# Cross attention's keys and values computed inside the third layer's mixer, with scores in five banks and keys feature-major

## The chip, the core and the metric

The kernel runs on one core of a Trainium2 chip. The metric is the device time of one launch in microseconds (us), the median of several runs. A core has five engines that run side by side, each through its own list of instructions in order, and that wait for one another by semaphores: TensorE (PE, matmul; PEld is its weight load), VectorE (DVE), ScalarE (ACT), GpSimd (POOL) and SyncE (SP, which here only issues the loads of weights). Matmul results land in PSUM, eight banks of 512 fp32 columns on 128 partitions; everything else lies in SBUF.

## What is computed

Three layers of a decoder over 512 tokens of width 1024, in fp32. The first two (A and B) are not touched by the change. The third, C, is the `second_block` of the reference:

```python
h = rms_norm_2(x, g_mix)
u, q, k, v, gate_logits = split(h @ w_in)
y_pool = causal_multiscale_pool(u, w_pool, pool_scale)
q, k = apply_rope(q), apply_rope(k)              # 4 heads x 2 halves of 64
o = diff_attention(q, k, v, lam)                 # softmax(half 0) - lam * softmax(half 1)
o = rms_norm_2(o, g_subln) * (1.0 - lam_init)
mixed = concatenate([y_pool, o]) * sigmoid(gate_logits)
x = x + mixed @ w_out
hc = rms_norm_2(x, g_cross)
mem_n = rms_norm_2(mem, g_mem)                   # 256 tokens of a memory
k, v = split(mem_n @ w_ckv)                      # 4 heads of 256
x = x + (softmax((hc @ w_cq) @ k.T) @ v) @ w_co
x = x + square(relu(rms_norm_2(x, g_mlp) @ w_up)) @ w_down
```

`mem_n @ w_ckv` needs nothing of x: its operands are inputs of the launch.

## The kernel before

All matrices of weights are cut into units of 1024 x 256 (1 MB), numbered in the order of `PHASES` (line 50). SP loads unit after unit into two buffers STG0 and STG1; ACT writes the high part of the unit (`split_hi`, WH) and DVE the rest (`split_lo`, WL), also into two buffers each. A product is three matmuls: high x high, low x high and high x low (`product`, line 472 is the matmul helper). A unit of a projection has 48 matmuls of 128x512. Semaphore `lo` says that a unit is split, `tile` that PE has finished a tile, `emptied_dve` or `emptied_act` that the tile's bank has been read. Unit u+2 can't be split until PE is through with unit u, and its load waits for the `lo` of unit u.

Layer C runs through the units C.u, C.qk, C.v, C.gate (in the projections DVE turns queries and keys by the rope), then the mixer (`layer_c_mixer`, no weights), then C.out, C.mem, C.cq, the cross attention, C.co and the MLP.

The mixer goes head by head, four heads h, with this chain for each:

- PE `scores(h, c)`: scores of half c, four query blocks of 128 (widths 128 to 512, 1280 columns), contraction over 64 rows. Half 0 lies in banks 0 to 2, half 1 in banks 3 to 5 (`1536 * c + DF_OFF[b]`). Of head 0 the two halves alternate, of the others all of half 0 comes first. The scores of half c of head h+1 wait until ACT has taken the exponentials of half c of head h.
- DVE `top(h, c)`: adds the causal mask, takes the row maxima, scales them (tile DMX).
- ACT exponentials (tile Y), with the row sums into DST.
- DVE difference: four scalar_tensor_tensor over Y.
- PE `turn(h, r)`: ten 128x128 transposes (line 1070) in three pieces r into bank 7; ACT copies each piece to UT; PE `apply(h, r)` multiplies by the values into bank 6.
- ACT copies the head to QC and its square to SQ.

Around it, four pooled groups (`UT,PAR` matmuls into banks 6 and 7, DVE scales them into GC_) fill the start; at the end 16 small matmuls sum the squares, and `head_factors` spreads the factors inside C.out's first unit, whose second half waits for the heads' operands.

C.mem has 8 units of 48 matmuls of 128x256: the memory's token tiles (MH2, ML2) are the stationary operand and the weights move, so the results are token-major. Units 0 to 3 are keys: ACT copies them to Y scaled by the tokens' factors, PE transposes them (line 1237) and ACT copies the transposes to CK. Units 4 to 7 are values, scaled by ACT into CV. The operand MH2, ML2 and the squares are made by ACT, DVE and POOL beside C.out, the operand of C.cq beside C.mem.

Of the kernel before, what the change touches and what calls it, by code (L numbers as in the profile page):

```python
# [26 lines left out]
F32R = mybir.dt.float32r  # L27
# [4 lines left out]
P = 128  # L32
# [20 lines left out]
    ("C.u", 2, "dve"), ("C.qk", 4, "dve"), ("C.v", 2, "dve"), ("C.gate", 4, "dve"), ("C.out", 4, "dve"),  # L53
    ("C.mem", 8, "act"), ("C.cq", 4, "dve"), ("C.co", 4, "dve"), ("C.mlp", 32, "dve"),
# [5 lines left out]
UNITS = len(KIND)  # L60

# [3 lines left out]
SPLITS = ["mem", "A.in", "A.mix", "A.mlp", "B.in", "B.mix", "B.mlp", "C.in", "C.mix", "mem2", "C.cross", "C.att", "C.mlp"]  # L65
# [41 lines left out]
rope_mm rope_sin rows_hi rows_in rows_tr rq rs rsc rv sb_a sb_az sb_cap sb_e sb_l sb_m sb_o sb_rc sb_sp sb_half sb_t sb_u sb_z  # L107
# [5 lines left out]
def program(nc, ws, xt_in, memt_in, memt2_in, par_in, con_in, rope_in, rcnt_in, out):  # L113
    ctx = ExitStack()
    with ctx:
# [40 lines left out]
        MX2 = KVM  # L156
        PS = ctx.enter_context(nc.psum_tensor("PS", [P, 8, 512], F32))
# [49 lines left out]
        with ExitStack() as sc:  # L207
            QC = sb("QC", [P, 4, S], scope=sc)
            KC = sb("KC", [P, 4, S], scope=sc)
            VC = sb("VC", [P, 4, NB, P], scope=sc)  # L210
            UT = sb("UT", [P, 4, 16 + S], scope=sc)
            GC_ = sb("GC_", [P, KD, S], scope=sc)
            COSIN = sb("COSIN", [P, 2, S], scope=sc)
            LAM = sb("LAM", [P, 8], scope=sc)
            PA = sb("PA", [P, 2, 16 + S], scope=sc)
            DST = sb("DST", [P, 5, 4 * NB], scope=sc)
            DMX = sb("DMX", [P, 2, 2, NB], scope=sc)
        with ExitStack() as sc:
            CQ0 = sb("CQ0", [P, 4, S], scope=sc)
            MH2 = sb("MH2", [P, KD, MEM], F32R, scope=sc)  # L220
            ML2 = sb("ML2", [P, KD, MEM], F32R, scope=sc)
        with ExitStack() as sc:
            CQ = sb("CQ", [P, KD, S], scope=sc)
            CQ_END = sb("CQ_END", [P, 4, S], scope=sc)
            CK = sb("CK", [P, KD, MEM], scope=sc)
            CV = sb("CV", [P, MB, D], scope=sc)
# [100 lines left out]
        NORMS = [n for n in SUMS if not n.startswith("mem")]  # L327
# [140 lines left out]
        def _(pe):  # L468
# [23 lines left out]
            def spread_tokens(name):  # L492

                pe.wait_ge(sems["rsc"], sums_done(name))
                for b in range(NB):
# [557 lines left out]
            def layer_c_mixer():  # L1053
                def scores(h, c):
                    pe.wait_ge(sems["df_exp"], 8 * (h - 1) + 4 * c + 4)
                    for b in (3, 2, 0, 1):
                        o = 1536 * c + DF_OFF[b]
                        last = mm(PSF[:, o:o + DF_WID[b]], QC[64 * c:64 * c + 64, h, b * P:(b + 1) * P],
                                  KC[64 * c:64 * c + 64, h, 0:DF_WID[b]], True, True)
                    last.then_inc(sems["df_s"], 1)  # L1060
# [25 lines left out]
                for b in (3, 2, 0, 1):  # L1086
                    for c in range(2):
                        o = 1536 * c + DF_OFF[b]
                        last = mm(PSF[:, o:o + DF_WID[b]], QC[64 * c:64 * c + 64, 0, b * P:(b + 1) * P],
                                  KC[64 * c:64 * c + 64, 0, 0:DF_WID[b]], True, True)  # L1090
                        if b == 1:
                            last.then_inc(sems["df_s"], 1)
                for g in range(4):
                    pe.wait_ge(sems["pool_z"], g + 1)
                    if g >= 2:
                        pe.wait_ge(sems["mixed"], g - 1)
                    elif g == 1:
                        pe.wait_ge(sems["rope_sin"], 8)
                    mm(PS[:, 6 + g % 2, :], par("w_pool", g * P, P), UT[:, g, 16:16 + S], True, True).then_inc(sems["pool_mm"], 1)
                for h in range(4):  # L1100
                    if h < 3:
                        scores(h + 1, 0)
                        scores(h + 1, 1)
# [8 lines left out]
                    apply(h, 2)  # L1112

                pe.wait_ge(sems["df_sq"], 4)
# [105 lines left out]
            rope_projection("C.gate", [[2, 3], [4, 5], [6, 7], []])  # L1220
# [3 lines left out]
            for r in range(4):  # L1224
                memory_rows(U0["C.mem"] + 2 * r, MH2, ML2, "mem2" if r == 0 else None)
                if r == 0:
                    sum_tokens("mem2", MB)
                memory_rows(U0["C.mem"] + 2 * r + 1, MH2, ML2)
                if r in (1, 2):

                    pr = r - 1
                    pe.wait_ge(sems["emptied_act"], emptied("act", U0["C.mem"] + 2 * pr + 1, 1))
                    if pr:
                        pe.wait_ge(sems["kv_t"], 4)
                    for f in range(4):
                        for t in range(MB):
# [1435 lines left out]
```

## Time and profile before

| | us |
|---|---|
| median of 3 runs | 2255.85 |
| range of the runs | 2253.93 to 2257.2 |
| the profiled execution | 2253.49 |
| its span in the trace | 2251.7 |
| PE busy, share of the span | 95% |
| DVE, ACT, POOL busy | 49%, 33%, 7% |

A stage's length is read from where PE's instructions begin and end. Start and length of each instruction are in microseconds from the span's start. Matmuls overlap, so the distance from start to start counts, not the length of one.

### The profile page before, as it was taken

How to read it: one execution, taken by the hardware profiler on the slowest of the kernel's cores; microseconds unless marked ns; L12 is line 12 of the kernel's file. 1: busy time of each engine (PE TensorE's matmuls, PEld its weight loads, DVE VectorE, ACT ScalarE, POOL GpSimd, SP SyncE). 2: the span in 40 equal slices, each digit the busy share in tenths (PEclk: the TensorE clock that was granted, in tenths of full speed). 3: DMA queues.
4: the chain of work that ended last, by engine and by line, in shares of the span. 5: the costliest groups of instructions: out<-in, count | busy, mean ns of one | idle time of the engine just before them, and what ended most of it. 6: DMA issues, size and time to landing. Idle time of an engine off the chain costs nothing.

```text
span 2251.7 us, 28790 instructions
## 1 busy us (share of the span) xinstructions
PE 2146.6 (95%) x11831; PEld 1757.9 (78%) x11831; DVE 1097.8 (49%) x1381; ACT 752.4 (33%) x1038; POOL 155.3 (7%) x137
## 2 busy tenths in 40 slices
PE   7999999899999999999999999899789999999998
PEld 6877888788888778767788888687469868888886
DVE  4664654454354353452744435555745334454453
ACT  5443432422122232673312213312435243222222
POOL 2000220200000210001100000300001001000001
PEclk9999999999999999999999999999889999999999
DMA  6231000122222222102222222322104302222221
GB/s 233 75 115 45 22 11 15 70 100 98 93 93 93 94 75 75 38 1 75 75 94 105 99 94 93 122 94 75 38 20 143 119 20 94 94 94 99 106 93 56
DMA packets 27025, 182.81 MB, mean 81 GB/s; under 512 B 2992, under 2 KB 3120, under 8 KB 5424
## 3 DMA queue, kind: packets, MB, share of 16 engines
q1 hardware_dynamic: 25200, 174.07, 21.8%
q10 hardware_dynamic: 1296, 4.71, 0.5%
q0 software_dynamic: 432, 2.62, 0.3%
q8 instruction: 74, 1.21, 0.2%
q14 instruction: 23, 0.19, 0.0%
HBM read 179.30 MB, written 2.10 MB: 81 GB/s over the span
## 4 chain that ended last, share of the span: by engine, by line
PE 86%; DVE 8%; ACT 3%; DMA 1%; issue 1%; POOL 0%; ACTq 0%; DVEq 0%; POOLq 0%; SPq 0%
PE PS L472 85%; ACT Y L1254 2%; DVE HL L1888 2%; DVE Y L1888 1%; DVE PS L1888 1%; DVE XT L1891 1%; DVE WL L1891 1%; ACT WH L1254 1%; DVE Y L1891 1%; DMA MX<-mem_t 0%; DVE SQ L1891 0%; PE PS L1070 0%; DMA STG<-weights 0%; PE PS L641 0%; POOL SQA L412 0%
## 5 line engine op out<-in xcount | busy, mean ns | idle before, releaser
L472 PE MATMUL PS<-HH,WH 128*128 128x512 f32 x1608 | 643.0, 400 | 32.4 <-DVE HL L1888 26.0
L472 PE MATMUL PS<-HL,WH 128*128 128x512 f32 x1608 | 632.1, 393 | 0.0
L472 PE MATMUL PS<-HH,WL 128*128 128x512 f32 x1608 | 631.6, 393 | 0.0
L1891 DVE TENSOR_TENSOR WL<-STG,WH 128x2048 fp32r<-128x2048 f32 (+1 forms) x167 | 376.3, 2253 | 286.5 <-ACT WH L1254 286.5
L1254 ACT ACTIVATE WH<-STG 128x2048 fp32r<-128x2048 f32 (+1 forms) x167 | 313.9, 1880 | 529.3 <-PE PS L472 527.8
L472 PEld LDWEIGHTS PS<-HH,WH 128*128 128x128 f32 x1608 | 305.4, 190 | 112.5 <-issue 28.7
L472 PEld LDWEIGHTS PS<-HH,WL 128*128 128x128 f32 x1608 | 305.4, 190 | 65.2
L472 PEld LDWEIGHTS PS<-HL,WH 128*128 128x128 f32 x1608 | 305.8, 190 | 62.7 <-issue 1.7
L472 PE MATMUL PS<-UPH,WH 128*128 128x512 f32 x768 | 299.1, 389 | 1.4 <-DVE UPL L1888 1.4
L472 PE MATMUL PS<-UPL,WH 128*128 128x512 f32 x768 | 298.8, 389 | 0.0
L472 PE MATMUL PS<-UPH,WL 128*128 128x512 f32 x768 | 298.8, 389 | 0.0
L472 PEld LDWEIGHTS PS<-UPH,WH 128*128 128x128 f32 x768 | 144.2, 188 | 31.6 <-DVE UPL L1888 1.8
L472 PEld LDWEIGHTS PS<-UPL,WH 128*128 128x128 f32 x768 | 144.2, 188 | 29.9
L472 PEld LDWEIGHTS PS<-UPH,WL 128*128 128x128 f32 x768 | 144.2, 188 | 29.9
L408 POOL TENSOR_TENSOR SQA<-SQ 128x512 f32<-128x512 f32 (+1 forms) x14 | 23.9, 1707 | 1695.6 <-ACT SQ L1254 1695.6
L1888 DVE SCALAR_TENSOR_TENSOR RR<-PS,RS 128x512 f32<-128x512 f32 x96 | 66.3, 691 | 152.6 <-PE PS L472 144.4
L1891 DVE TENSOR_TENSOR Y<-Y,PS 128x512 f32<-128x512 f32 x64 | 43.9, 687 | 180.2 <-PE PS L472 180.2
L1254 ACT ACTIVATE UPH<-RR 128x512 fp32r<-128x512 f32 x64 | 40.5, 632 | 233.5 <-DVE RR L1888 233.5
L1891 DVE TENSOR_TENSOR XT<-XT,PS 128x512 f32<-128x512 f32 x80 | 54.4, 682 | 125.9 <-PE PS L472 125.9
L412 POOL TENSOR_TENSOR SQA<-SQA,SQ 128x512 f32<-128x512 f32 (+1 forms) x70 | 94.8, 1354 | 134.9 <-ACT SQ L1254 131.0
L1254 ACT ACTIVATE Y<-PS 128x512 f32<-128x512 f32 (+5 forms) x96 | 61.6, 646 | 85.1 <-PE PS L472 70.3
L472 PE MATMUL PS<-WH,MH 128*128 128x256 f32 x192 | 56.3, 293 | 12.6 <-DVE ML L1888 9.2
(291 smaller groups left out, 2127.2 us busy)
## 6 DMA issues: line engine op xcount, KB each, us to landing
STG<-weights SPq DMA_DIRECT2D x163, 1024.0 KB, 4.8
XT<-x_t ACTq DMA_DIRECT2D x2, 1024.0 KB, 12.4
out_t<-Y SPq DMA_DIRECT2D x8, 256.0 KB, 2.0
STG<-weights SPq DMA_DIRECT2D x4, 256.0 KB, 5.7
MX<-mem_t ACTq DMA_DIRECT2D x4, 256.0 KB, 8.3
CON<-consts ACTq DMA_DIRECT2D x1, 1024.0 KB, 17.2
Y<-recip_counts POOLq DMA_DIRECT2D x1, 1024.0 KB, 5.1
KVM<-mem_t POOLq DMA_DIRECT2D x1, 1024.0 KB, 7.2
```

Of the source, the lines that this page charges most:

```text
L408: pool.tensor_tensor(SQA[:, 0:n], SQ[:, base % 4, 0:n], SQ[:, (base + 1) % 4, 0:n], ALU.add).then_inc(sems["sqa"], 1)
L412: pool.tensor_tensor(SQA[:, 0:n], SQA[:, 0:n], SQ[:, (base + k) % 4, 0:n], ALU.add).then_inc(sems["sqa"], 1)
L472: return pe.matmul(o, l, r, start=start, stop=stop, **kw)
L1254: return act.activation(o, i, f, **kw)
L1888: return dve.scalar_tensor_tensor(out=o, in0=a, scalar=s_, in1=b, op0=op0, op1=op1)
L1891: return dve.tensor_tensor(o, a, b, op)
```

## The change

Units are numbered so that C.mem comes before C.out. Each of its 16 half units (`memory_part(r, t)`, 24 matmuls of 128x256) stands in PE's list between steps of the mixer and writes its half of bank 5: both parts of unit 0 between the pooled groups, the first part of unit 1 ahead of head 1's scores and the second after `turn(0, 0)`; from head 1 on one part of unit 2h+1 after `turn(h, 0)` and the other after `apply(h, 0)`; unit 2h+2 at the head's end.

- Scores: half 0 and 1 together fill banks 0 to 4, so both halves of a head are issued as one alternating group that waits until all exponentials of the head before are taken; `top` and the exponentials wait for both halves.
- Keys: the weights are the stationary operand and the memory moves (units 0 to 3), so that keys come out feature-major. DVE scales them by a row of factors RS2 straight into CK; the 16 transposes and ACT's copies of them go.
- The memory's norm (squares, sums, root, the new row of factors) runs beside C.gate; MH2 and ML2 now lie in the upper half of HH and HL and are made right after C.gate, ahead of the mixer's first `top` on DVE and the first exponentials on ACT.
- The splits of the units stand in ACT's and DVE's mixer lists: two per head.
- C.cross's operand goes to UPH, UPL and is made beside C.out, two tiles a unit.

```diff
-    ("C.u", 2, "dve"), ("C.qk", 4, "dve"), ("C.v", 2, "dve"), ("C.gate", 4, "dve"), ("C.out", 4, "dve"),
-    ("C.mem", 8, "act"), ("C.cq", 4, "dve"), ("C.co", 4, "dve"), ("C.mlp", 32, "dve"),
+    ("C.u", 2, "dve"), ("C.qk", 4, "dve"), ("C.v", 2, "dve"), ("C.gate", 4, "dve"), ("C.mem", 8, "act"),
+    ("C.out", 4, "dve"), ("C.cq", 4, "dve"), ("C.co", 4, "dve"), ("C.mlp", 32, "dve"),
...
+        def score_at(c, b):
+            return DF_OFF[b] + (0 if c == 0 else 256 if b == 1 else 1536)
...
+                def scores(h):
+                    if h:
+                        pe.wait_ge(sems["df_exp"], 8 * h)
+                    for c, b in ((0, 1), (1, 3), (0, 3), (1, 2), (0, 2), (1, 0), (0, 0), (1, 1)):
...
+                def memory_part(r, t):
...
+                        if r < 4:
+                            mm(out, WH[s][:, k, c], MH2[:, k, :], k == 0, False)
+                            mm(out, WH[s][:, k, c], ML2[:, k, :], False, False)
+                            last = mm(out, WL[s][:, k, c], MH2[:, k, :], False, k == KD - 1)
+                        else:
+                            mm(out, MH2[:, k, c], WH[s][:, k, :], k == 0, False)
+                            mm(out, ML2[:, k, c], WH[s][:, k, :], False, False)
+                            last = mm(out, MH2[:, k, c], WL[s][:, k, :], False, k == KD - 1)
...
                 for h in range(4):
+                    if h == 0:
+                        memory_part(1, 0)
                     if h < 3:
-                        scores(h + 1, 0)
-                        scores(h + 1, 1)
+                        scores(h + 1)
                     pe.wait_ge(sems["df_a"], 4 * h + 4)
                     if h == 0:
                         pe.wait_ge(sems["mixed"], 4)
                     turn(h, 0)
+                    memory_part(2 * h + 1, 0 if h else 1)
                     turn(h, 1)
                     apply(h, 0)
+                    if h:
+                        memory_part(2 * h + 1, 1)
                     turn(h, 2)
                     apply(h, 1)
                     apply(h, 2)
+                    if h < 3:
+                        memory_part(2 * h + 2, 0)
+                        memory_part(2 * h + 2, 1)
...
+            operand_lo("mem2", MX2, "g_mem", MH2, ML2, MEM)
             dve.wait_ge(sems["lam_act"], 1)
...
+            def memory_keys(r):
+                dve.wait_ge(sems["tile"], 2 * (U0["C.mem"] + r) + 2)
+                dve.wait_ge(sems["rs"], copies_done("mem2"))
+                tt(CK[:, 2 * r:2 * r + 2, :], PS[:, 5, :].rearrange("p (f n) -> p f n", f=2),
+                   RS2[:, :].unsqueeze(1).to_broadcast([P, 2, MEM]), ALU.mult).then_inc(sems["emptied_dve"], 2)
...
+            for h in range(4):
+                if h == 1:
+                    memory_keys(2)
                 if h < 3:
                     top(h + 1, 0)
                     top(h + 1, 1)
+                split_lo(U0["C.mem"] + 2 * h + 2)
+                if h < 2:
+                    memory_keys(2 * h + 1)
+                if h < 3:
+                    difference(h + 1)
+                split_lo(U0["C.mem"] + 2 * h + 3)
```

PE's list in the first head, before: from the last scores of head 1 to the head's last product. CON,Y are the transposes (`turn`), UT,VC the products with the values (`apply`).

```order
L1070 MATMUL PS<-CON,Y 128x128 [waits mixed,df_a]
L1070 MATMUL PS<-CON,Y 128x128 x3
L1070 MATMUL PS<-CON,Y 128x128 [waits df_at]
L1070 MATMUL PS<-CON,Y 128x128 x3
L472 MATMUL PS<-UT,VC 128x512 [waits df_at]
L1070 MATMUL PS<-CON,Y 128x128 [waits df_at]
L1070 MATMUL PS<-CON,Y 128x128
L472 MATMUL PS<-UT,VC 128x384 [waits df_at]
```

PE's list now at the same place; HH and HL with 128x256 are the memory's operand, a part has eight such threes.

```order
L474 MATMUL PS<-KC,QC 128x256 [waits df_b]
L1105 MATMUL PS<-CON,Y 128x128 [waits mixed,df_a]
L1105 MATMUL PS<-CON,Y 128x128 x3
L474 MATMUL PS<-HH,WH1 128x256
L474 MATMUL PS<-HL,WH1 128x256
L474 MATMUL PS<-HH,WL1 128x256
...
L1105 MATMUL PS<-CON,Y 128x128 [waits df_at]
L1105 MATMUL PS<-CON,Y 128x128 x3
L474 MATMUL PS<-UT,VC 128x512 [waits df_at]
```

A part of a memory unit now stands between the first and the second piece of transposes.

DVE's list at the start of the mixer, before: the last split of a unit, then the lambda of the differential attention (LAM).

```order
L1891 TENSOR_TENSOR GC_<-PS,RS 128x512 [waits tile] x2
L1891 TENSOR_TENSOR WL1<-STG1,WH1 128x2048 [waits hi]
L1891 TENSOR_TENSOR LAM<-LAM 128x1 [waits lam_act]
L2474 TENSOR_SCALAR LAM<-LAM 128x1 [waits lam]
```

And now, up to the first `top`:

```order
L1931 TENSOR_TENSOR GC_<-PS,RS 128x512 [waits tile] x2
L1931 TENSOR_TENSOR WL1<-STG1,WH1 128x2048 [waits hi]
L1928 SCALAR_TENSOR_TENSOR HL<-KVM,PAR,HH 128x256 [waits hh] x8
L1931 TENSOR_TENSOR LAM<-LAM 128x1 [waits lam_act]
L2517 TENSOR_SCALAR LAM<-LAM 128x1 [waits lam]
L1931 TENSOR_TENSOR PS<-PS,CON 128x3x128 [waits df_s]
L1931 TENSOR_TENSOR PS<-PS,CON 128x128
```

Eight instructions for the memory's low part have come between the split and the first mask.

ACT's list at the mixer's end, before (the last head):

```order
L1254 ACTIVATE UT<-PS 128x512 [waits df_o,df_tr]
L1254 ACTIVATE UT<-PS 128x512 [waits df_tr]
L1254 ACTIVATE UT<-PS 128x256 [waits df_tr]
L1254 ACTIVATE QC<-PS 128x512 [waits df_o]
L1254 ACTIVATE SQ<-PS 128x512
```

And now; KVM holds the memory's values (CV):

```order
L1275 ACTIVATE KVM<-PS,RSC 128x256 [waits rsc,tile]
L1275 ACTIVATE KVM<-PS,RSC 128x256
L1275 ACTIVATE WH0<-STG0 128x2048 [waits tile,load0]
L1275 ACTIVATE UT<-PS 128x512 [waits df_o,df_tr]
L1275 ACTIVATE UT<-PS 128x512 [waits df_tr]
L1275 ACTIVATE KVM<-PS,RSC 128x256 [waits rsc,tile]
L1275 ACTIVATE KVM<-PS,RSC 128x256
L1275 ACTIVATE UT<-PS 128x256 [waits df_tr]
L1275 ACTIVATE WH1<-STG1 128x2048 [waits tile,load1]
L1275 ACTIVATE QC<-PS 128x512 [waits df_o]
L1275 ACTIVATE SQ<-PS 128x512
```

A split of a unit of C.out has come between the last piece of transposes and the copy and square that end the mixer.

## Rows read from the trace of the kernel before

**Rows 1.** The page: the span, the chain that ended last by engine, a DMA issue.

```profile
span 2251.7 us, 28790 instructions
...
PE 86%; DVE 8%; ACT 3%; DMA 1%; issue 1%; POOL 0%; ACTq 0%; DVEq 0%; POOLq 0%; SPq 0%
...
STG<-weights SPq DMA_DIRECT2D x163, 1024.0 KB, 4.8
```

**Rows 2.** Busy times by stage: mixer, C.out's first unit, C.mem.

```profile
core 0: us, PE busy (x) PEld busy (x) DVE busy (x) ACT busy (x) POOL busy (x), PEclk, DMA share, GB/s
1583.20:1653.60 70.40, 50.15 (x177) 29.81 (x177) 38.02 (x93) 34.34 (x93) 0.00 (x0) 0.76 0.04 15
1653.60:1671.10 17.50, 15.97 (x76) 12.89 (x77) 8.76 (x16) 2.83 (x5) 0.00 (x0) 0.90 0.00 1
1704.87:1754.10 49.23, 48.95 (x409) 48.70 (x408) 30.62 (x18) 32.02 (x44) 10.32 (x6) 1.00 0.43 150
```

**Rows 3.** The same view in stretches of 5 us inside the mixer.

```profile
1600.00:1605.00 5.00, 3.54 (x18) 1.99 (x16) 4.89 (x13) 0.19 (x2) 0.00 (x0) 1.00 0.00 0
...
1625.00:1630.00 5.00, 4.31 (x13) 2.47 (x12) 4.90 (x15) 0.60 (x1) 0.00 (x0) 0.50 0.00 0
...
1640.00:1645.00 5.00, 4.31 (x13) 2.74 (x14) 0.02 (x1) 1.20 (x2) 0.00 (x0) 0.50 0.00 0
```

**Rows 4.** PE in order of time in the mixer: start, length, idle before and its releaser.

```profile
1584.03 2.43 PE L472 MATMUL PS<-KC,QC 64*128 64x512 f32 x16 [0.83 <-issue]
1586.39 1.98 PE L472 MATMUL PS<-UT,PAR 128*128 128x512 f32 x4
1594.96 3.75 PE L472 MATMUL PS<-UT,PAR 128*128 128x512 f32 x4 [6.58 <-DVE GC_ L1888]
1598.64 4.24 PE L472 MATMUL PS<-KC,QC 64*128 64x512 f32 x16
...
1615.63 0.66 PE L1070 MATMUL PS<-CON,Y 128*128 128x128 f32 x4
1616.97 0.66 PE L1070 MATMUL PS<-CON,Y 128*128 128x128 f32 x4 [0.69 <-ACT UT L1254]
...
1618.60 1.47 PE L472 MATMUL PS<-UT,VC 128*128 128x384 f32 x6
```

**Rows 5.** DVE, then ACT, in order of time: two tops, a difference, two halves' exponentials.

```profile
1588.89 0.75 DVE L1891 TENSOR_TENSOR PS<-PS,CON 128x384 f32<-128x384 f32 x2
...
1591.48 0.76 DVE L1891 TENSOR_TENSOR PS<-PS,CON 128x384 f32<-128x384 f32 x2
...
1602.29 1.94 DVE L1888 SCALAR_TENSOR_TENSOR Y<-Y,DST 128x128 f32<-128x128 f32 x4
...
1608.95 0.36 ACT L1254 ACTIVATE Y<-PS,DMX 128x128 f32<-128x128 f32 x1
...
1610.96 0.39 ACT L1254 ACTIVATE Y<-PS,DMX 128x128 f32<-128x128 f32 x1
```

**Rows 6.** Instructions by tile, ns min/median/max: ML, WH and WL.

```profile
L1888 DVE SCALAR_TENSOR_TENSOR ML<-MX,PAR,MH x8: 476/479/487, 8.6 to 14.5; 128x256 fp32r<-128x256 f32 x8
L1888 DVE SCALAR_TENSOR_TENSOR ML<-KVM,PAR,MH x8: 473/956/965, 1676.7 to 1682.3; 128x256 fp32r<-128x256 f32 x8
...
L1254 ACT ACTIVATE WH<-STG x12: 1892/1910/1926, 1584.5 to 1748.9; 128x2048 fp32r<-128x2048 f32 x12
...
L1891 DVE TENSOR_TENSOR WL<-STG,WH x12: 2279/2293/2293, 1586.4 to 1750.9; 128x2048 fp32r<-128x2048 f32 x12
```

**Rows 7.** PE in order of time: a token sum in C.mem, a spread in C.cq.

```profile
1710.63 0.50 PE L472 MATMUL PS<-CON,SQA 128*128 128x1 f32 x4
...
1711.44 0.36 PE L472 MATMUL PS<-WH,MH 128*128 128x256 f32 x1
...
1772.31 1.05 PE L472 MATMUL PS<-CON,RSC 128*128 128x128 f32 x8
```

**Rows 8.** PE in order of time: the mixer's last sums and the start of C.out.

```profile
1648.45 5.33 PE L472 MATMUL PS<-CON,SQ 128*128 128x1 f32 x32 [1.17 <-ACT SQ L1254]
1653.64 0.77 PE L472 MATMUL PS<-HH,WH 128*128 128x512 f32 x1
```

More of the change, by code:

```diff
@@ L156, in program @@
         MX2 = KVM
+        MH2, ML2 = (t[:, 4:8, :].rearrange("p a (c n) -> p (a c) n", c=2) for t in (HH, HL))
+        CV = KVM[:, :, :].rearrange("p k n -> p (k n)").rearrange("p (t d) -> p t d", t=MB)
         PS = ctx.enter_context(nc.psum_tensor("PS", [P, 8, 512], F32))
@@ L544, in product, with projection @@
                         beside(8 * j + KD - 1)
-            def projection(name, split=None, norm=None, after=None, halfway=None, order=range(KD), behind=None):
+            def projection(name, split=None, norm=None, after=None, halfway=None, order=range(KD), behind=None, x=(HH, HL)):
                 def fn(u, i, step):
@@ L1804, in gate_sig, with memory_norm @@
                 A(GC_[:, k, :], GC_[:, k, :], ACT.Sigmoid).then_inc(sems["sig"], 1)
-            units("C.gate", evac=gate_sig)
+            def memory_norm(r):
+                if r == 0:
+                    act.wait_ge(sems["mem2_in"], 16)
+                    for k in range(KD):
+                        square("mem2", k, MX2[:, k, :], MEM)
+                elif r == 1:
+                    root("mem2", MB)
+                elif r == 2:
+                    act.wait_ge(sems["bc"], bcast_done("mem2"))
+                    A(RS2[:, :], PS[:, 4, 0:MEM], ACT.Copy).then_inc(sems["rs"], 1)
+            units("C.gate", evac=gate_sig, behind=memory_norm)
             act.wait_ge(sems["lam"], 2)
             A(LAM[:, 2:4], LAM[:, 0:2], ACT.Exp).then_inc(sems["lam_act"], 1)
-            act.wait_ge(sems["tile"], 2 * U0["C.out"])
+            act.wait_ge(sems["tile"], 2 * U0["C.mem"])
+            for k in range(KD):
+                A(MH2[:, k, :], MX2[:, k, :], ACT.Copy, scale=par("g_mem", k)).then_inc(sems["hh"], 1)
             def exponentials(h, c):
-                act.wait_ge(sems["df_nm"], 2 * h + c + 1)
+                act.wait_ge(sems["df_nm"], 2 * h + 2)
                 if c:
@@ L2488, in top, with pooled @@
                 dve.tensor_scalar(DMX[:, c, 1, :], DMX[:, c, 0, :], -(64 ** -0.5), None, ALU.mult).then_inc(sems["df_nm"], 1)
-            top(0, 0)
-            top(0, 1)
-            for g in range(4):
+            def pooled(g):
                 dve.wait_ge(sems["pool_mm"], g + 1)
@@ L2512, in _ @@
                         .then_inc(sems["df_a"], 1)
+            top(0, 0)
+            top(0, 1)
+            pooled(0)
+            pooled(1)
+            memory_keys(0)
+            pooled(2)
+            pooled(3)
+            for g in range(4):
+                mix_lo("C.mix", g, GC_[:, g, :])
+            dve.wait_ge(sems["lam"], 4)
+            difference(0)
+            for h in range(4):
+                if h == 1:
+                    memory_keys(2)
                 if h < 3:
```

201 lines of the change are left out of this document (101 added, 100 removed).

## The prediction, made before the changed kernel ran

> **What bounds the kernel now.** I read the page's chain first: PE holds 86% of it [rows 1], so time goes only where PE's work shrinks or PE stops waiting. Next the busy times by stage. In C.mem PE is busy 48.95 us of 49.23, and its weight loads 48.70 [rows 2]: with 256 moving columns the loads alone fill the stage, so nothing can be squeezed there, only moved. In the mixer PE is busy 50.15 us of 70.40 at a mean clock of 0.76 [rows 2], while DVE has 38 us of work and ACT 34: nobody is full, each head is a chain of hand-overs. Its 20 us of idle time, and the time lost to the lower clock, are the cover that the change wants to use. The order of time shows it: PE idles 6.58 us before the third pooled group [rows 4], and four short matmul groups at half clock take 3.75 us where the same work took 1.98.
>
> **The change part by part.** The sum goes against the profiled execution (2253.49 us, 2.4 below the median of 2255.85); the difference is then put on the median.
>
> *Removed: the stage C.mem*, 49.2 us of PE. It has 409 rows: 384 matmuls of 128x256, 16 for the transposes, 8 for the token sum and one neighbour. The token sum takes 0.8 us (from 1710.63 to 1711.44) [rows 7], 16 transposes twice the 0.8 us that eight records of the same shape take (1772.31) [rows 7], with their waits 1.9. So 46.5 us are parts, 2.9 us for each of the 16. A part keeps its 24 matmuls, sizes and loads whichever operand is stationary: 2.9 us at full clock. The transposes and ACT's copies go for good.
>
> *Added to C.gate*: the token sum (0.8) and one spread of half the width of the row at 1772.31 (0.5): +1.3 us. Squares, root and RS2 lie on ACT, DVE and POOL, which have slack in a projection.
>
> *The mixer, walked anew.* Before it takes 70.4 us from the last C.gate matmul to the first of C.out. Now:
>
> 1. First scores and two pooled groups as before, to 1588.4 [rows 4].
> 2. DVE makes ML2 ahead of the first top: 8 instructions. Beside POOL they took 956 ns each, with POOL idle 479 [rows 6]; in the mixer POOL does nothing [rows 2], and pipelined (about 0.08 apart less than their length) 8 are 3.2 us. ACT's eight MH2 copies run in step. Everything behind moves by 3.2: the first difference, which ended at 1604.2 (1602.29 + 1.94) [rows 5], ends at 1607.4. Unit 0 and the first part of unit 1 (8.7 us of PE) lie in the idle time before it, beside the 6.58 us and what follows. DVE's read of unit 0 lies beside the exponentials.
> 3. Head 0: the first transposes and a part of unit 1 end by 1611. The head's last product needs ACT's third copy, which now stands behind the exponentials of head 1's half 0, and these wait for both tops: 1607.4 + 2 x 2.6 (a top, start to start) + 2.0 (a half's exponentials) + 0.4 + 0.5 [rows 5] = 1615.5. Unit 2 follows: 5.8, to 1621.3.
> 4. Heads 1 and 2. PE's own work per head: scores 2.4, if alternating halves always take what head 0's did (2.43) and not the 4.24 of head 1's one half after the other at full clock [rows 4]; transposes and products 3.7 (from 1615.63 to 1620.07 less the 0.69 of waiting) [rows 4]; four parts 11.6. Together 17.7. The others need less: DVE two tops 5.2, difference 2.3, two splits 4.6, keys 0.7, which is 12.8; ACT two splits 3.8, exponentials 4.1, copies 1.3 for UT and 1.1 for QC and SQ, values 0.9, which is 11.2 [rows 5, 6]. The ring of scores, tops and exponentials is 2.4 + 5.2 + 4.1 = 11.7. So PE is the bound, and both heads end at 1621.3 + 35.4 = 1656.7. Loads: that of unit 4 can start at about 1614.5, when DVE is through with unit 2, and lands 4.8 us later [rows 1], 2 us before ACT wants it; the others have more.
> 5. Head 3: 3.7 + 5.8, plus 0.9 until ACT has emptied the one bank of unit 6, to 1667.1. ACT then has a split of C.out (1.9) [rows 6] ahead of the last copy and square (1.1): 1669.3, partly beside the last products.
> 6. The last sums: 5.2 us at a low clock (1648.45 to 1653.64) [rows 8]; eight such records took 0.8 at full clock [rows 7], so 32 take 3.2. C.out starts at 1672.5.
>
> That is 89.3 us, and 2.0 for about twenty hand-overs and a spell of low clock in the first head: 91.3 for 70.4, +20.9.
>
> *C.out*: its first unit ran at 0.90 [rows 2], from a slow start (24 matmuls in 7.2 us, the later pace gives 5.4). If PE comes in at full clock: -1.9. The operand of C.cq, now made beside C.out, is two tiles a unit; the last is ready 4 us after C.out ends, and C.cq's first unit asks for it after 42 of 48 matmuls, 9.5 us in. Hidden.
>
> Sum: -49.2 + 1.3 + 20.9 - 1.9 = **-28.9 us**; 2255.85 - 28.9 = 2227.
>
> *A rule against a row.* PE was busy 4.31 us of 5 from 1625 to 1630 and again from 1640 to 1645, and the clock was granted at 0.50 in both, while from 1600 to 1605 with 3.54 busy it was 1.00 [rows 3]. So in the mixer a busy PE was no warrant of the full clock. The Trainium skill ("TensorE: Matmul & The Clock Gate", Part 1: The HAM clock gate) says that the clock has two states, that the lower is the default and that activity releases it. By that rule the denser mixer would run at full clock and the sum is the one above; by the rows at 0.50 it could stay low, which is the second rival.
>
> The bounds of what no row shows: a part at half clock takes 1.9 times as long (3.75 to 1.98 for the same pooled matmuls [rows 4]), 5.5 us for 2.9. ML2 costs 6.2 us instead of 3.2 if the longer duration holds, the scores 4.24 instead of 2.43 if they don't overlap: +3 and +5.4. The other way, the 2.0 allowance and up to 3 us of step 5's tail may fall away.
>
> **The rivals.**
>
> *Hand-overs stay on PE's path.* Each head has five places where PE waits for ACT or DVE (three copies, the difference, the emptied bank 5). I take them as covered by parts; if 2.5 to 3 us of each head's are not, four heads cost +11: 2238. For it: one bank for all parts, ACT in strict order with splits between copies. Against: the slack of 5 us a head on both engines in step 4.
>
> *The clock stays low, slower than before.* At half clock the 16 parts cost 16 x 2.6 = 41.6 us more, and the scores, transposes and products of four heads about 0.9 x (2.4 + 3.7) x 4 = 22 less what step 6 and C.out already have: in all some +58, the kernel then 2285. It turns slower than before when half of the mixer (28.9 of 58) runs at 0.50. For it: the two rows at 0.50. Against: those stretches held half-array scores and waits; now 16 dense bursts stand between. A quarter to a third of the mixer at 0.50 would give +15 to +19, 2244.
>
> *Better than forecast.* PE at full clock throughout, no loss in head 0, the tail hidden: -5, 2222.
>
> *It doesn't move what it says*: if the loads came late (unit 4 has 2 us of slack) PE would wait 2 to 3 us once or twice; this stays within the first rival.
>
> **How the numbers follow.** Chances: the forecast (2224 to 2232) 45%, better (2218 to 2224) 14%, hand-overs (2232 to 2241) 25%, part of the mixer at the low clock (2241 to 2251) 10%, low clock throughout or a loss past 2260: 4%, about even: 2%. The range from 2219 to 2243 leaves out about 2 in 10. A measurement of this kernel can tell 0.2%, 4.5 us, from no change: faster 0.94, same 0.02, slower 0.04.
>
> **What would show it.** Right: the stage from C.gate's end to C.out's start near 91 us with PE busy over 90% and a mean clock over 0.95; heads 1 and 2 each 17.7 us from scores to scores; a part 2.9 us; scores 2.4 us in every head; ML2 479 ns each; no wait at C.cq's start. Wrong: a clock under 0.85 in the mixer; waits of PE for ACT's UT or DVE's WL inside the heads of over 2 us each; C.cq waiting for UPL.

## The result, and the profile after

| | before | changed |
|---|---|---|
| median, us | 2255.07 | 2229.98 |
| range of the runs, us | 2253.93 to 2257.2 | 2224.48 to 2231.18 |
| the profiled execution, us | 2253.49 | 2229.99 |
| its span, us | 2251.7 | 2228.2 |

The ratio of the changed kernel to the one before is 0.9883, with a 95% interval of 0.9865 to 0.9901: 25.1 us less, where 28.9 were forecast. 2229.98 lies 3 us above the forecast of 2227.0 and inside the range.

The page of the changed kernel, its span, PE's busy time, and the chain that ended last by engine, to be held against [rows 1]:

```profile
span 2228.2 us, 28766 instructions
...
PE 2134.8 (96%) x11819; PEld 1754.3 (79%) x11819; DVE 1096.9 (49%) x1385; ACT 750.1 (34%) x1029; POOL 157.7 (7%) x137
...
PE 87%; DVE 8%; ACT 3%; issue 1%; DMA 0%; POOL 0%; ACTq 0%; DVEq 0%; POOLq 0%; SPq 0%
```

Next the busy times of the changed kernel by stretch, to be held against [rows 2]: the mixer, its last sums, C.out's first unit, three pieces from the sums into C.out, and the piece around the third pooled group. The number after the engines is the granted clock, as a share of the full one.

```profile
core 0: us, PE busy (x) PEld busy (x) DVE busy (x) ACT busy (x) POOL busy (x), PEclk, DMA share, GB/s
1591.10:1682.20 91.10, 81.72 (x561) 70.97 (x560) 61.67 (x113) 54.82 (x117) 0.00 (x0) 0.96 0.29 105
1676.40:1682.20 5.80, 5.73 (x32) 5.76 (x32) 1.49 (x2) 1.27 (x1) 0.00 (x0) 0.60 0.54 184
1682.20:1699.00 16.80, 15.25 (x69) 12.21 (x69) 8.08 (x15) 2.82 (x5) 0.00 (x0) 0.83 0.00 0
1677.00:1680.00 3.00, 3.00 (x19) 3.00 (x18) 0.89 (x2) 0.67 (x1) 0.00 (x0) 0.60 0.36 76
1680.00:1683.00 3.00, 3.00 (x14) 2.90 (x14) 0.35 (x2) 0.06 (x1) 0.00 (x0) 0.50 0.68 279
1683.00:1686.00 3.00, 3.00 (x9) 2.32 (x8) 0.43 (x2) 0.25 (x1) 0.00 (x0) 0.50 0.00 0
...
1606.00:1609.00 3.00, 2.96 (x5) 1.44 (x5) 1.90 (x3) 3.00 (x13) 0.00 (x0) 0.50 0.02 5
```

The mixer grew from 70.4 to 91.1 us, and PE's busy time in it from 50.15 to 81.72, while the mean clock rose from 0.76 to 0.96. The idle time fell from 20 us to 9.4. The clock goes down twice: for the third pooled group, behind a gap of 2.71 us, and at the mixer's end, where it stays down into C.out.

PE in order of time, the changed kernel, to be held against [rows 4] and [rows 8]. CON,Y are the transposes, UT,VC the products with the values, CON,SQ the sums of squares, and WH, WL with HH, HL and 128x256 the parts. The scores, the pooled products, the products with the values and the sums stand in the trace as two records for each matmul of the program, so x32 is the 16 sums. The transposes and the matmuls of the parts and of C.out have one record each.

```profile
1591.94 2.43 PE L474 MATMUL PS<-KC,QC 64*128 64x256 f32 x16 [0.83 <-issue]
1594.30 1.98 PE L474 MATMUL PS<-UT,PAR 128*128 128x512 f32 x4
1597.17 0.36 PE L474 MATMUL PS<-HH,WH 128*128 128x256 f32 x1 [0.89 <-DVE HL L1928]
...
1606.04 3.58 PE L474 MATMUL PS<-UT,PAR 128*128 128x512 f32 x4 [2.71 <-DVE GC_ L1928]
...
1615.20 0.66 PE L1105 MATMUL PS<-CON,Y 128*128 128x128 f32 x4 [0.34 <-DVE Y L1928]
...
1622.83 0.70 PE L474 MATMUL PS<-UT,VC 128*128 128x256 f32 x2 [1.68 <-ACT UT L1275]
1623.27 0.38 PE L474 MATMUL PS<-HH,WH 128*128 128x256 f32 x1
...
1629.21 2.43 PE L474 MATMUL PS<-KC,QC 64*128 64x256 f32 x16
...
1646.46 2.43 PE L474 MATMUL PS<-KC,QC 64*128 64x256 f32 x16
...
1664.00 0.60 PE L1105 MATMUL PS<-CON,Y 128*128 128x128 f32 x4
1665.18 0.36 PE L474 MATMUL PS<-WH,HH 128*128 128x256 f32 x1 [0.58 <-ACT KVM L1275]
...
1676.47 5.94 PE L474 MATMUL PS<-CON,SQ 128*128 128x1 f32 x32 [2.12 <-issue]
1682.27 0.77 PE L474 MATMUL PS<-HH,WH 128*128 128x512 f32 x1
...
1690.42 0.83 PE L474 MATMUL PS<-CON,DST 128*128 128x128 f32 x6
```

Of the 6.58 us of idle time before the third pooled group 0.89 and 2.71 are left, with unit 0 between them. From head 1's turn to head 3's PE doesn't stop: no row there has a wait. Then come 0.58 us ahead of unit 7 and 2.12 us ahead of the last sums, and behind them C.out's first 24 matmuls take 8.15 us (from 1682.27 to 1690.42) where before they took 7.2.

The experiments are compared by three distances: from the first scores to C.out's first matmul (90.3 us in the changed kernel), from there to CON,DST, the spread of the heads' factors that stands behind C.out's first 24 matmuls (8.15), and both together (98.5).

### The profile page after: what moved, and what is told of

The parts are those of the page before. It is cut to its first block, busy times and chain, and to the rows that moved or that the text cites. A ratio compares the mean times of both kernels' runs of the same rounds, so it can differ in the third digit from the quotient of the medians.

```text
span 2228.2 us, 28766 instructions
## 1 busy us (share of the span) xinstructions
PE 2134.8 (96%) x11819; PEld 1754.3 (79%) x11819; DVE 1096.9 (49%) x1385; ACT 750.1 (34%) x1029; POOL 157.7 (7%) x137
## 4 chain that ended last, share of the span: by engine, by line
PE 87%; DVE 8%; ACT 3%; issue 1%; DMA 0%; POOL 0%; ACTq 0%; DVEq 0%; POOLq 0%; SPq 0%
PE PS L474 85%; DVE HL L1928 1%; ACT Y L1275 1%; DVE PS L1928 1%; DVE Y L1928 1%; DVE XT L1931 1%; DVE WL L1931 1%; DVE Y L1931 1%; ACT WH L1275 1%; DVE SQ L1931 0%; DMA STG<-weights 0%; PE PS L643 0%; DVE DMX L2531 0%; POOL SQA L414 0%; DVE HL L1931 0%
## 5 line engine op out<-in xcount | busy, mean ns | idle before, releaser
L474 PE MATMUL PS<-HH,WH 128*128 128x512 f32 (+1 forms) x1608 | 637.6, 396 | 33.5 <-DVE HL L1928 26.8
L474 PE MATMUL PS<-HL,WH 128*128 128x512 f32 (+1 forms) x1608 | 624.6, 388 | 0.0
L474 PE MATMUL PS<-HH,WL 128*128 128x512 f32 (+1 forms) x1608 | 624.3, 388 | 0.0
L474 PE MATMUL PS<-UPH,WH 128*128 128x512 f32 x832 | 324.2, 390 | 1.4 <-DVE UPL L1928 1.4
L474 PE MATMUL PS<-UPH,WL 128*128 128x512 f32 x832 | 323.7, 389 | 0.0
L474 PE MATMUL PS<-UPL,WH 128*128 128x512 f32 x832 | 323.7, 389 | 0.0
L474 PEld LDWEIGHTS PS<-UPH,WH 128*128 128x128 f32 x832 | 156.2, 188 | 34.0 <-DVE UPL L1928 1.8
L474 PEld LDWEIGHTS PS<-UPH,WL 128*128 128x128 f32 x832 | 156.2, 188 | 32.5
L474 PEld LDWEIGHTS PS<-UPL,WH 128*128 128x128 f32 x832 | 156.2, 188 | 32.3
L1931 DVE TENSOR_TENSOR RQ<-RR 128x512 f32<-128x512 f32 x96 | 66.5, 692 | 3.3
```

What stands on the lines that cost most here:

```text
L474: return pe.matmul(o, l, r, start=start, stop=stop, **kw)
L1931: return dve.tensor_tensor(o, a, b, op)
```

## The experiments

The theory is the prediction's: the gain is the idle time and the low clock of the mixer, filled with parts, and it hangs on the order of the scores and on ACT's order at the tail. Against it stand a gain from the other pieces of the change (the order of the scores, the feature-major keys, the edit in layer A) and, for the tail, two causes of the low clock: the gap ahead of the sums, or the sums themselves. The kernel before, measured beside the experiments, stood at 2255.84, 2256.26 and 2253.40 us.

**Parts in a block.** All parts behind the heads, nothing between a head's steps; the new order of the scores, the feature-major keys and all that lies outside the mixer stay.

```diff
-                memory_part(0, 0)
-                memory_part(0, 1)
                 pooled(2)
...
-                    memory_part(2 * h + 1, 0 if h else 1)
...
-                        memory_part(2 * h + 2, 0)
-                        memory_part(2 * h + 2, 1)
+                for r in range(8):
+                    memory_part(r, 0)
+                    memory_part(r, 1)
```

> The changed kernel, but all 16 half units of the memory stand in one block behind the mixer's four heads (ACT's and DVE's splits, keys and values behind their head loops, results alternating between banks 5 and 4); the keys stay feature-major, the norm stays beside C.gate, the scores stay alternating. Theory (the gain is PE's idle time inside the mixer filled with parts): the heads take as long as before, some 60 to 65 us, plus 46.5 of block, so gate's end to C.out's start is 112 to 118 us for 91.1, and the launch takes 2250 to 2256. Rival (most of the gain comes from the transposes that went, the norm and C.cq's operand made elsewhere, and the alternating scores): 2235 to 2242.

Measured: 2261.57 us, ratio 1.0024 [1.0008, 1.0041]. The whole gain is gone, and the launch lies 5.6 us above the 2250 to 2256 that were expected. Its busy times, of the heads and of the block, and its waits of PE from the gate's end to C.out (engine, line, what it waited for, us, times, longest):

```profile
1588.28:1659.98 71.70, 40.24 (x145) 23.84 (x145) 41.24 (x100) 34.79 (x98) 0.00 (x0) 0.72 0.04 15
1659.98:1706.70 46.72, 46.72 (x386) 46.43 (x384) 18.81 (x11) 16.67 (x15) 0.00 (x0) 0.99 0.39 136
...
PE PS L474 <- ACT UT L1268: 10.1, 3, 3.9
PE PS L474 <- DVE GC_ L1919: 9.8, 1, 9.8
PE PS L1105 <- DVE Y L1919: 6.3, 2, 3.3
```

The block takes 46.7 us, where 46.5 were reckoned for the parts of C.mem. C.mem took 49.2 before, so the other pieces save 2.5 us there; but the heads take 71.7 up to the block, where before they took 65.3 up to the last sums. What the change saves is therefore saved by the place of the parts. From the gate's end to C.out it takes 123.0 us, 5 more than the 118 that were expected at most, and the rows say where. The wait before the third pooled group is 9.8 us for 6.58, as ML2 comes first. And PE waits up to 3.9 us for the third copy of UT, which in ACT's list stands behind exponentials that wait for both tops. That the second is the price of scores and tops that come as one group is read from these rows; no run takes it alone. In the changed kernel the parts hide it except in head 0.

**Halves in turn.** The scores of half 0 first, then those of half 1, all else as in the changed kernel.

```diff
-                    for c, b in ((0, 1), (1, 3), (0, 3), (1, 2), (0, 2), (1, 0), (0, 0), (1, 1)):
+                    for c, b in ((0, 1), (0, 3), (0, 2), (0, 0), (1, 3), (1, 2), (1, 0), (1, 1)):
```

> The changed kernel with each head's scores issued one half after the other (order 1, 3, 2, 0 of half 0, then 3, 2, 0, 1 of half 1), nothing else. Theory (PE is the bound in heads 1 to 3, and only alternating halves overlap in the array): each head's scores take 4.2 us for 2.4, and from head 1's scores to the mixer's end +1.8 for each of heads 1 to 3, +5.4 in all, a little less if head 1's lie beside DVE's difference: launch +3.6 to +5.4. Rival (the scores' length is hidden behind hand-overs, or order doesn't matter): below +1.

Measured: 2232.92 us, ratio 0.9906 [0.9882, 0.9930]. That is 2.9 us above the changed kernel, less than the 3.6 to 5.4 expected, and the intervals overlap; the trace has to tell. Two heads' scores:

```profile
1627.69 3.82 PE L474 MATMUL PS<-KC,QC 64*128 64x256 f32 x16
...
1646.33 3.82 PE L474 MATMUL PS<-KC,QC 64*128 64x256 f32 x16
```

The same 16 records take 3.82 us in place of 2.43 (4.2 were expected), and the round of a head takes 18.64 in place of 17.25: the 1.39 us come through whole, and PE has no wait in these heads. From the first scores to C.out it is 94.9 in place of 90.3. Half 0 lies in rows 0 to 63 of both operands and half 1 in rows 64 to 127. The Trainium skill ("TensorE: Matmul & The Clock Gate", Part 3: Packing small matmuls) says that matmuls of fewer rows run at once where they lie in different groups of rows; the trace agrees, with a factor of 1.57 for two halves of 64 rows.

**Last part behind.** The second part of unit 7 goes behind head 3's products, and with it, in ACT's list, the last copies of the values and the split of C.out's unit go behind the last copy and square.

```diff
-                    if h:
+                    if h in (1, 2):
                         memory_part(2 * h + 1, 1)
...
-                pe.wait_ge(sems["emptied_act"], emptied("act", U0["C.mem"] + 7, 1))
+                memory_part(7, 1)
...
```

> The changed kernel, but the last half unit of the memory stands behind head 3's last product instead of between its transposes, and ACT takes the last values and the split of C.out's second unit behind the head's copy and square (the wait for bank 5 moves to C.out's factors). PE then has 2.9 us of dense matmuls where it idled 2.1 us. Theory (the clock fell in that gap, and with it the last sums took 5.8 us for 3.2 and C.out's first 24 matmuls 8.15 for 5.45): heads' end to the sums' start shrinks by 2 to 3 us and the sums and C.out's start run at full clock: gate's end to C.out's start 84 to 86 us for 91.1, C.out's first unit 14 for 16.7, launch -7 to -9. Rival (the 16 matmuls of one column lower the clock by themselves): only -2 to -4, with sums of 5 us or more.

Measured: 2228.00 us, ratio 0.9864 [0.9834, 0.9894]: 2.0 us below the changed kernel, where 7 to 9 were expected. PE and the granted clock at the tail:

```profile
1679.49 3.99 PE L474 MATMUL PS<-CON,SQ 128*128 128x1 f32 x32
1683.35 0.77 PE L474 MATMUL PS<-HH,WH 128*128 128x512 f32 x1
...
1680.00:1682.00 2.00, 2.00 (x20) 2.00 (x20) 0.00 (x0) 2.00 (x3) 0.00 (x0) 1.00 0.00 0
1682.00:1684.00 2.00, 2.00 (x13) 1.90 (x13) 1.64 (x1) 1.61 (x2) 0.00 (x0) 0.65 0.03 8
1684.00:1686.00 2.00, 2.00 (x6) 1.57 (x5) 1.45 (x6) 0.31 (x1) 0.00 (x0) 0.50 0.20 25
```

The gap of 2.12 us is gone and the sums take 3.9 us (3.2 were expected), so C.out starts 85.4 us after the first scores in place of 90.3. But C.out's first 24 matmuls still take 8.4 us (1683.35 to 1691.75), not 5.45. The theory that the gap alone took C.out's clock has fallen: here PE is busy without a pause, 2.00 of 2.00 in each row, and the clock drops to 0.50 all the same, behind the 16 sums. The rival had the sums as the cause, which is what is left, but wanted 5 us or more for them. To CON,DST it takes 93.9 us for 98.5; that the launch shows less of it is the clock elsewhere (PE came to C.gate's first matmul at 1546.33, 6 us later than in the changed kernel).

**Gap filled.** Ten matmuls of 128x512 into a free bank stand in the gap; they compute nothing that is used.

```diff
+                pe.wait_ge(sems["df_exp"], 32)
+                pe.wait_ge(sems["hl"], split_done("C.mix", 3))
+                for n in range(10):
+                    mm(PS[:, 0, :], HH[:, 0, 0:P], HH[:, n % 4, :], True, True)
                 pe.wait_ge(sems["df_sq"], 4)
```

> The changed kernel with ten idle-time matmuls of 128x512 into a free bank ahead of the wait for the last square (their result is not used). They last 2.3 us, about as long as the gap of 2.1 us. Theory (the gap lets the clock fall): sums 3.2 us for 5.8 and C.out's first 24 matmuls 5.45 for 8.15, launch -4 to -5. Rival (the one-column matmuls do it, or the clock falls for another reason): sums stay at 5 us or more, launch 0 to +0.5.

Measured: 2224.43 us, ratio 0.9866 [0.9845, 0.9888]. The tail:

```profile
1673.05 2.66 PE L474 MATMUL PS<-HH 128*128 128x512 f32 x10
1675.56 3.66 PE L474 MATMUL PS<-CON,SQ 128*128 128x1 f32 x32
1679.08 0.48 PE L474 MATMUL PS<-HH,WH 128*128 128x512 f32 x1
...
1676.00:1680.00 4.00, 4.00 (x33) 3.87 (x34) 1.29 (x4) 0.99 (x2) 0.00 (x0) 1.00 0.48 150
1680.00:1682.00 2.00, 2.00 (x7) 1.57 (x6) 0.43 (x2) 0.05 (x1) 0.00 (x0) 0.52 0.58 234
```

The sums fall from 5.8 us to 3.5, so the gap did cost them the clock. C.out's first 24 take 7.16 (1679.08 to 1686.24), not the 5.45 of the theory, and the clock is at 0.52 behind the sums again. With the gap the clock falls during the sums, without it behind them; so the gap sets when it falls, but isn't needed for the fall. To CON,DST it is 95.3 us for 98.5, so of the launch's 5.5 us the tail explains 3.2.

**Sums among dense matmuls.** As the last part behind, and the sums of heads 0 to 2 stand in pairs between the steps of that last part; only head 3's come after it.

```diff
...
+                def early_sums(k):
+                    if k < 6:
+                        square_sum(2 * k)
+                        square_sum(2 * k + 1)
...
+                pe.wait_ge(sems["df_sq"], 3)
+                memory_part(7, 1, early_sums)
                 pe.wait_ge(sems["df_sq"], 4)
+                for n in range(12, 16):
+                    last = square_sum(n)
```

> The kernel of e3 (last part behind the last product), with the twelve one-column matmuls of heads 0 to 2 put between the 24 matmuls of that last part, so that only the four of head 3 stand alone ahead of C.out. In e3 the clock fell at about 1683, 3 us after the sixteen one-column matmuls began, with PE busy all the time. Theory formed from it (a row of one-column matmuls lowers the clock, whether PE idles ahead of it or not): no low clock at C.out's start, its first 24 matmuls take 5.4 to 5.6 us for 8.4, launch -3 against e3, the sums themselves as long as before. Rival (the clock falls there for another reason, in step with something else): C.out's first 24 matmuls stay at 7 us or more, launch as e3.

Measured: 2225.07 us, ratio 0.9864 [0.9828, 0.9900]. The last sums, C.out's start, the spread behind it, and the clock of the two stretches:

```profile
1678.80 0.95 PE L474 MATMUL PS<-CON,SQ 128*128 128x1 f32 x8
1679.61 0.47 PE L474 MATMUL PS<-HH,WH 128*128 128x512 f32 x1
...
1685.61 1.57 PE L474 MATMUL PS<-CON,DST 128*128 128x128 f32 x12 [0.26 <-DVE DST L1944]
...
1673.00:1680.00 7.00, 7.00 (x60) 6.91 (x60) 0.00 (x0) 2.08 (x5) 0.00 (x0) 1.00 0.34 137
1679.61:1685.61 6.00, 5.74 (x27) 4.44 (x26) 3.23 (x6) 3.63 (x4) 0.00 (x0) 1.00 0.08 22
```

With the same matmuls in another order the clock stays at 1.00 and C.out's first 24 take 5.7 us and 0.26 of a new wait for the factors. In all nine profiles with the sums in a row they took 7.2 to 8.4; in the four with spread sums (this kernel and three that follow) 5.7. From the first scores to CON,DST it is 91.2 us, for 93.9 in the kernel with the last part behind and 98.5 in the changed one: 4.6 of the 7.3 come from the place of the last part, 2.7 from the place of the sums. Against the changed kernel the launch gained 4.9 in the median, with single runs from 2216.35 to 2231.42, so the size of this gain rests on the trace.

**Start reordered.** The kernel above, and head 1's scores now stand ahead of the first part of unit 1, and DVE's low part of the pooled groups behind the two tops of head 1.

```diff
                     if h < 3:
                         scores(h + 1)
+                    if h == 0:
+                        memory_part(1, 0)
...
-            for g in range(4):
-                mix_lo("C.mix", g, GC_[:, g, :])
...
+                if h == 0:
+                    for g in range(4):
+                        mix_lo("C.mix", g, GC_[:, g, :])
                 if h < 3:
                     difference(h + 1)
```

> The kernel of e5, with the start of the mixer in another order: head 1's scores ahead of the first part of unit 1 on PE, and on DVE the low halves of the four pooled tiles behind the keys of unit 1 instead of ahead of the first difference. In the changed kernel the first difference ended at 1615.1 after 2.5 us of these, head 0's last product waited 1.7 us for ACT, and unit 2 started at 1623.3, held by DVE's split and keys. Theory (DVE bounds the mixer up to unit 2): from the first scores to unit 2's start 29.0 us for 31.4, launch -2.4 against e5. Rival (something else is as late, ACT's copy or the scores): above -0.8.

Measured: 2220.53 us, ratio 0.9838 [0.9811, 0.9865]. Where head 0 ends:

```profile
1620.88 0.70 PE L474 MATMUL PS<-UT,VC 128*128 128x256 f32 x2 [1.00 <-ACT UT L1286]
1621.23 0.47 PE L474 MATMUL PS<-HH,WH 128*128 128x256 f32 x1
```

From the first scores (1591.03) to unit 2 it takes 30.2 us in place of 31.3 in the changed kernel: only half of what was expected, since the copy of UT still comes 1.0 us late. To CON,DST it takes 90.3 us, 0.9 less than with the sums among dense matmuls, nearer to the rival's 0.8 than to the 2.4 of the theory. The launch is 4.5 us shorter than that kernel's; the trace gives 0.9 of them to this edit.

**Before, with the change's edit in layer A.** The change also moves a count in layer A from its own semaphore to another. The edit alone, on the kernel before:

```diff
-                    A(ROWS_HI.bitcast(F32R), PS[0:64, 5, P:4 * P], ACT.Copy).then_inc(sems["rows_hi"], 1)
+                    A(ROWS_HI.bitcast(F32R), PS[0:64, 5, P:4 * P], ACT.Copy).then_inc(sems["sc_act"], 1)
```

> The kernel before with the only edit that the change makes to layer A: ACT's copy of the turned rows counts on sc_act instead of on a semaphore of its own, and the two waits of DVE are renumbered. In the profiles the changed kernel came to C.gate 6.9 us later than the kernel before, through stretches of low clock from 210 to 250 us in code that is otherwise the same. Theory (the clock falls in another place from execution to execution, for no reason in the code): launch within 2 us of before, and the profile comes to C.gate anywhere between 1533 and 1546. Rival (the edit moves something in layer A): launch +4 to +7.

Measured: 2252.86 us, ratio 0.9990 [0.9971, 1.0009]. The edit costs nothing that can be told. Its profile shows something else, the mixer of the kernel before a second time:

```profile
1586.90:1653.50 66.60, 45.73 (x177) 27.34 (x177) 38.03 (x93) 34.30 (x93) 0.00 (x0) 0.82 0.05 16
```

With the same code and a mean clock of 0.82 in place of 0.76 it took 66.6 us in place of 70.4 [rows 2]. The old mixer's length varies with the clock by 3.8 us, so the 20.8 us that the mixer grew would be some 24.5 against this profile.

**The changed kernel again.**

> The changed kernel once more, unchanged, beside the others on this chip, to see how far its profile differs from the first in layers A and B and after C.cq. Theory (the clock's spells differ from execution to execution): C.gate reached between 1533 and 1546, the mixer from C.gate's end to C.out's start again 91.1 to within 0.5. Rival (a kernel's spells are its own): C.gate at 1540.4 to within 1 us, the low stretches again at 210 to 250.

Measured: 2231.60 us, ratio 0.9900 [0.9878, 0.9921]. As far as two profiles tell, the rival was right: PE comes to C.gate at 1540.54, after 1540.37 in the first profile. From the first scores (1592.09) to C.out (1682.36) it is 90.3 us once more, and the low clock from 205 to 255 us is there again with the same 0.83.

**The changed kernel without the edit in layer A**, and **the best kernel** (the one with the start reordered) **without it**:

> The changed kernel with one thing put back: in layer A the copy into ROWS_HI counts on its own semaphore rows_hi again, as in the kernel before (the change had folded it into sc_act, one number later for DVE). Nothing else. In the profiles of the changed kernel PE came to C.gate 6.85 us later than in the kernel before, and the granted clock from 205 to 255 us was 0.83 where before had 1.00. Theory: the edit costs nothing; the spells of low clock move with small shifts of time in code that is the same. Then the time stays within the changed kernel's own spread, 2224 to 2234, and what differs from the changed kernel before C.gate is in the granted clock alone, with no new wait of PE; the clock from 205 to 255 may be anything from 0.83 to 1.00. Rival: the edit moves DVE's or ACT's work in layer A so that PE loses its clock there each time; then the clock from 205 to 255 is 1.00 again, PE comes to C.gate about 7 us earlier and the time is 2223 to 2225.

> The same put back in the kernel of e6_start_reordered (sums of squares among the last part's matmuls, last part behind the products, mix_lo later, first part of unit 1 behind head 1's scores). Theory (edit costs nothing): 2216 to 2224, the mixer as in e6, 85.3 us from C.gate's last matmul to C.out's start. Rival (the edit costs about 3 us by the clock from 205 to 255, 0.93 in e6): 2217 and a clock of 1.00 there.

Measured: 2228.14 us, ratio 0.9888 [0.9856, 0.9920], and 2217.99 us, ratio 0.9852 [0.9822, 0.9882]. Both lie in what a free edit allows; for the second the time alone decides nothing, as the rival had 2217. The clock from 205 to 255 us was 0.93 in both, where the rival wanted 1.00.

**The best kernel again, with the edit.**

> The kernel of e6_start_reordered once more, in five rounds, for a narrower interval: it stood at 2220.53 with 0.9838 [0.9811, 0.9865], the changed kernel at 2229.98 and 2231.6. By the traces it wins 5.9 us in the mixer and 2.4 us in C.out's first 24 matmuls against the changed kernel, 8.3 in all: theory 2222 plus or minus 2, ratio 0.984 to 0.9865. Rival: the rest of its lead was a spread of the clock in layers A and B; then 2224 to 2227, ratio over 0.9865.

Measured: 2220.29 us, ratio 0.9849 [0.9821, 0.9877]. It keeps its lead of about 10 us over the changed kernel, 8.2 of them from the first scores to CON,DST, where it takes 90.3 us for the third time. Here the clock from 205 to 255 us was 1.00 with the edit in place. With the edit the value was 0.83, 0.90, 0.93 or 1.00 by the kernel and without it 0.93, 0.93 and 1.00: the edit is not what decides.

One view shows where the clock parts. Before, changed and last kernel at the same work of layer A, stretches of 2 us (16 records of one column stand from 208.86, 208.06 and 212.95 us on):

```profile
208.00:210.00 2.00, 2.00 (x15) 1.82 (x15) 0.86 (x2) 0.00 (x0) 0.00 (x0) 1.00 0.00 0
210.00:212.00 2.00, 2.00 (x15) 1.60 (x15) 0.00 (x0) 0.00 (x0) 0.00 (x0) 1.00 0.00 0
...
208.00:210.00 2.00, 2.00 (x19) 1.96 (x18) 0.23 (x2) 0.00 (x0) 0.00 (x0) 0.97 0.00 0
210.00:212.00 2.00, 2.00 (x7) 1.34 (x6) 0.00 (x0) 0.00 (x0) 0.00 (x0) 0.50 0.00 0
...
212.00:214.00 2.00, 2.00 (x16) 1.72 (x14) 0.86 (x2) 0.00 (x0) 0.00 (x0) 1.00 0.00 0
214.00:216.00 2.00, 2.00 (x16) 1.60 (x15) 0.00 (x0) 0.00 (x0) 0.00 (x0) 1.00 0.00 0
```

In all three PE is busy without a pause; behind the same one-column sums the clock drops in the changed kernel (second pair) and holds in the others (first and third), where the sums stand 0.8 and 4.9 us later. No run takes the sums of layer A away, so that they bring the drop there isn't shown, nor why it comes at one time and not at the other. The Trainium skill ("TensorE: Matmul & The Clock Gate", Part 1) says that the chip's monitor runs freely and isn't tied to the kernel's start, so that one kernel can show different numbers of slow matmuls from run to run; the traces fit that across kernels, and so do the single runs of one kernel (with the last part behind: 2231.28, 2230.24, 2225.76 and 2216.32 us at mean clocks of 0.978, 0.978, 0.981 and 0.984), though the two profiles of the changed kernel show the drop at the same place.

## Why the prediction was right, and where not

*C.mem removed, gate longer.* -49.2 and +1.3, as forecast: the token sum in C.gate took 0.8 us and the spread 0.45 (from C.gate's first matmul to its last it is 1.05 more). That the parts cost as much in a row as in C.mem shows in the 46.7 us of the block.

*The mixer.* 91.3 was forecast and 91.2 measured, but two errors cancel in it, so the match is in part luck. The mean clock was 0.96 for the "over 0.95" of the prediction and PE busy for 89.7% (81.72 of 91.10) for its "over 90%", a hair under. By the steps:

- Step 2 (ML2 in 3.2 us): 3.25, at 477 ns each, the value with POOL idle [rows 6].
- Steps 2 and 3, head 0: the first difference ends 3.0 us later after the gate than before, for the 3.2 forecast. The last product waits 1.68 us for the third copy of UT as step 3 said, and unit 2 starts 32.2 us behind the gate's end for 32.3.
- Step 4: 17.25 us from scores to scores and 17.5 to head 3, for 17.7; scores 2.43 in every head, parts 2.95 to 3.0.
- Step 5: the wait for the emptied bank was 0.58 for 0.9; ACT's split ahead of the last copy left a gap of 2.12 us on PE. Up to the sums it took 85.4 us for 86.1.
- Step 6: the sums took 5.8 us for 3.2. This term was mis-sized: it took the pace of eight records in dense work for 32 in a row behind a gap. The 2.0 us allowed for hand-overs weren't needed up to the sums and happened to pay for most of it.

*C.out's start* is the second term that was mis-sized: -1.9 forecast, +1.0 measured (8.15 us for 7.2). The step assumed that a mixer at full clock hands the full clock on. It did up to the gap of 2.12 us; behind it the clock was still 1.00 from 1676 to 1677 and 0.50 from 1678. The filled gap took 2.3 us off the sums and left C.out's start at 7.16; the spread sums brought it to 5.7. The gap, the pace of the sums and C.out's start are together the 7.3 us (98.5 to 91.2) that the kernel with the sums among dense matmuls saves.

*C.cq* has no wait at its start, as forecast; PE waits for nothing from 1725 to 1760.

From the first matmul of C.gate to the token sum of C.cq, the same instruction in both kernels:

```profile
1533.52 0.48 PE L472 MATMUL PS<-HH,WH 128*128 128x512 f32 x1
...
1765.02 0.95 PE L472 MATMUL PS<-CON,SQA 128*128 128x1 f32 x8
...
1540.37 0.48 PE L474 MATMUL PS<-HH,WH 128*128 128x512 f32 x1
...
1745.38 0.95 PE L474 MATMUL PS<-CON,SQA 128*128 128x1 f32 x8
```

Before (the first two) it is 231.5 us, now 205.0: -26.5 for the -28.9 forecast, and the 2.4 that are missing are the 2.9 of C.out's start but for 0.5. The rest of the way is the same code but for the edit in layer A. There the profiled execution lost 6.9 us ahead of C.gate and won 3.9 behind that token sum, with the same waits of PE in both kernels to within 1 us and another clock (0.83 for 1.00 from 205 to 255 us; 0.99 for 0.98 behind the token sum). That makes -23.5 for the two profiled executions, where the medians differ by 25.1. The sum of the prediction had no term for it. In the second profile of the kernel before, with the shorter mixer, the same stretch took 227.8 us: against that one the change gives -22.8 there, so the -26.5 too holds only to the clock's 3 to 4 us.

*The rivals.* Hand-overs stayed on PE's path only up to the end of head 0 (0.89, 2.71, 0.34 and 1.68 us) and at the tail. The clock that stays low, the rival on the other side, did not come about. The PE at 0.50 for 4.31 us busy of 5 [rows 3] belonged to a stage with gaps: the block experiment has 0.72 in its heads, so the low clock comes back when the parts go. Within the mixer the rule of the Trainium skill ("TensorE: Matmul & The Clock Gate", Part 1) that activity releases the clock was the better guide than those rows. At the one-column sums the rows were: a busy PE is no warrant.

## To carry to other kernels

Work that needs nothing from its surroundings can fill an engine that waits in a chain of hand-overs, as long as the chain's other engines have room for its splits and copies: 16 parts that hold PE for 46.5 us lengthened the mixer by 20.8 here. Try such parts also around matmuls of very few columns, and not only in gaps: the 16 one-column sums in a row cost C.out's start 1.5 to 2.7 us that they didn't cost among dense matmuls. When a tail is costed, take the clock from what PE does in it, not from what it did before.

## What the runs showed of the hardware

- Behind one-column matmuls in a row the granted clock fell although PE counts as busy. At the mixer's tail it was 1.00, then 0.65, then 0.50, with no idle time, and it stayed 1.00 in the four kernels where dense matmuls stood between the same sums. In layer A it was 0.97, then 0.50, behind such a row in the changed kernel, and 1.00 behind the same row in two others.
- A gap of 2.12 us ahead of the 16 sums made them take 5.8 us where they took 3.5 with the gap filled.
- Two halves of 64 rows in turns of single matmuls take 2.43 us, one half after the other 3.82, for the same 16 records.
- The same scalar_tensor_tensor of 128x256 took 956 ns beside POOL [rows 6] and 477 with POOL idle.
- The granted clock in code that no edit touches differs from kernel to kernel, which moves a launch by several us: PE came to C.gate at 1533.52 before and at 1540.37 in the changed kernel, and between 1533.00 and 1546.33 over all thirteen profiles. The same code of the old mixer took 66.6 and 70.4 us. A difference of 3 us between two of these kernels says little unless the trace shows its place.
